# Two attentions of a two-block transformer on row halves of the array, with other places for a head's extras and a token-major key norm

## The reference

```python
s = einsum("bqhcd,bkhcd->bhcqk", q, k) * 64 ** -0.5
p = softmax(s)
w = p[:, :, 0] - lam * p[:, :, 1]
o = einsum("bhqk,bkhd->bqhd", w, v)                # v: 128 wide
o = o * rsqrt(mean(o * o) + 1e-5) * g * (1 - lam_init)
```

```python
q, k = rms_norm(heads(a_q), q_norm_g), rms_norm(heads(a_k), k_norm_g)
outs, lses = zip(*[dilated_window_attention(q, k, v, rel_bias, w, d) for w, d in DILATED_PATTERNS])
```

## Time and profile before

| | before |
|---|---|
| median of 3 runs | 2809.41 us (2808.64 to 2809.75) |
| profiled execution: time, span | 2811.53 us, 2809.7 us |
| mean granted PE clock | 0.963 |
| PE / DVE / ACT / POOL busy | 89% / 38% / 21% / 2% |
| instructions | 23563 |

### The profile page before, as it was taken

How to read it: one execution, slowest core, us unless ns; L and a number is a source line. 1 busy time by engine, 2 the same in 40 slices (tenths; PEclk the granted TensorE clock), 3 DMA queues, 4 the chain that set the end, 5 groups by cost and what they waited for, 6 DMA issues and landing times.

```text
span 2809.7 us, 23563 instructions
## 1 busy us (share of the span) xinstructions
PE 2507.4 (89%) x9789; PEld 1379.9 (49%) x9789; DVE 1059.4 (38%) x1759; ACT 581.7 (21%) x912; POOL 54.2 (2%) x75
## 2 busy tenths in 40 slices
PE   6899998889999779999899989789888897979888
PEld 2344544458888648888645455433223232323323
DVE  3353346346665576665456673400101010110101
ACT  1110115332332242332234242300000000000000
POOL 2000000000000100000000000000000000000000
PEclk9999999899999889999899999899999999999999
DMA  8050231035554215554110110499999999999998
GB/s 325 0 179 16 67 107 73 0 114 201 192 181 154 71 64 200 190 188 138 63 47 31 44 33 7 195 382 413 401 405 396 409 406 411 393 414 398 404 405 339
DMA packets 184545, 594.22 MB, mean 211 GB/s; under 512 B 12450, under 2 KB 13984, under 8 KB 167926
## 3 DMA queue, kind: packets, MB, share of 16 engines
q1 hardware_dynamic: 180482, 581.14, 54.3%
q0 software_dynamic: 3648, 11.44, 1.2%
q10 hardware_dynamic: 308, 0.13, 0.0%
HBM read 590.54 MB, written 2.13 MB: 211 GB/s over the span
## 4 chain that ended last, share of the span: by engine, by line
PE 68%; DMA 18%; DVE 9%; ACT 3%; SPq 1%; issue 1%; POOL 0%; ACTq 0%; DVEq 0%
PE PS L611 12%; PE PS L784 8%; PE PS L786 8%; PE PS L785 8%; PE PS L149 7%; PE PS L1008 7%; DMA RING<-in_w_up_dram 6%; PE PS L992 5%; DMA RING<-in_w_gate_dram 3%; PE PS L1022 2%; DMA AT_e<-in_w_up_dram 2%; PE PS L524 2%; PE PS L687 2%; DMA HID_e<-in_w_up_dram 1%; DMA AT_e<-in_w_gate_dram 1%; PE PS L915 1%
## 5 line engine op out<-in xcount | busy, mean ns | idle before, releaser
L992 PE MATMUL PS<-RING,HID_e 128*64 128x512 f32 x1280 | 331.5, 597 | 66.7 <-DMA RING<-in_w_up_dram 39.1
L2125 DVE TENSOR_TENSOR TMP<-TMP,PS 128x512 f32<-128x512 f32 x32 | 20.6, 684 | 567.7 <-PE PS L992 567.7
L992 PEld LDWEIGHTS PS<-RING,HID_e 128*64 128x64 f32 x1280 | 104.0, 136 | 262.2 <-issue 139.6
L1490 DVE SCALAR_TENSOR_TENSOR TMP<-RING,MODC,TMP 128x512 f32<-128x512 f32 x224 | 168.4, 752 | 19.3 <-ACT TMP L1099 10.0
L1008 PE MATMUL PS<-RING,HID_e 128*64 128x512 f32 x632 | 155.7, 594 | 2.5 <-DMA RING<-in_w_down_dram 2.5
L611 PE MATMUL PS<-AT_a,RING 128*128 128x512 f32 x320 | 140.7, 598 | 0.0
L992 PE MATMUL PS<-XT,HID_e 128*64 128x512 f32 x312 | 106.8, 597 | 14.8 <-DMA XT<-in_w_up_dram 7.5
L992 PE MATMUL PS<-AT_e,HID_e 128*64 128x512 f32 x296 | 104.3, 597 | 15.9 <-DMA AT_e<-in_w_up_dram 9.9
L611 PE MATMUL PS<-AT_e,RING 128*128 128x512 f32 x256 | 111.9, 593 | 0.0
L784 PE MATMUL PS<-AH_b,WH_b 128*128 128x512 f32 x256 | 101.2, 395 | 3.6 <-DVE AL_b L1539 3.6
L784 PE MATMUL PS<-AH_d,WH_d 128*128 128x512 f32 x256 | 101.4, 396 | 3.3 <-DVE AL_d L1539 3.2
(11 more groups left out here) (415 smaller groups left out, 3960.5 us busy)
## 6 DMA issues: line engine op xcount, KB each, us to landing
RING<-in_w_gate_dram SPq DMA_DIRECT2D x82, 1024.0 KB, 17.2
RING<-in_w_down_dram SPq DMA_DIRECT2D x79, 1024.0 KB, 22.7
RING<-in_w_up_dram SPq DMA_DIRECT2D x78, 1024.0 KB, 18.5
RING<-in_mlp_w_dram SPq DMA_DIRECT2D x64, 1024.0 KB, 5.4
RING<-in_ada_w_dram SPq DMA_DIRECT2D x48, 1024.0 KB, 5.3
RING<-in_w_ada_dram SPq DMA_DIRECT2D x24, 1024.0 KB, 5.1
XT<-in_w_up_dram SPq DMA_DIRECT2D x21, 1024.0 KB, 18.5
AT_e<-in_w_down_dram SPq DMA_DIRECT2D x21, 1024.0 KB, 21.2
```

The source lines that it names most:

```text
L992: last = pe.matmul(b[64 * d:64 * d + 64, :], xv_[:, k, 64 * d:64 * d + 64], wv, start=k == 0, stop=k == 7)
L1490: dve.scalar_tensor_tensor(out=ada_tmp, in0=ring.view("ada", which, cb, k // 4)[:, k % 4, :], scalar=sil[:, c0 + step * k:c0 + step * k + ...
```

## The change

In the differential attention the queries are stored once (`Qf`); the scores of half c use array rows 64c to 64c+63, and the order of the four matmuls alternates between the halves, with a wait of PE on its own matmul where two halves share a bank. lam is stored negated; the mix takes p0 + p1 * (-lam * s0 / s1) without dividing by s0, and the epsilon of the norm is multiplied by s0 squared instead (guard, mean). Values, sums, root, reciprocal and spread, scale are placed at steps 1, 2, 3 of the next head and 0, 1 of the one after that.

In the dilated attention keys are projected first, with tokens on partitions; their norm is 8 values per token, applied in a broadcast multiplication, and four transposes and an ACT copy with the product of both gains bring them back. The queries are copied as they are; their row sums (matmuls with two columns) give 128x8 row scales, which the logit operation takes as a per-row scalar in place of 0.125. A step s is now a pair of heads and 128 queries: two logit matmuls on row halves, two logit operations and maxima, one negation, two exponentials, one reciprocal. Logits run two steps ahead, with four buffers. The values of a pair come channel-major from column halves (8 matmuls of 512 columns), the reciprocals are broadcast by 8 matmuls and copied by ACT, and one DVE product writes the out-projection's input; so the final transposes, copies and the 32 scalings are gone. On SP the keys' weights are loaded ahead of the queries'; POOL loads the biases into four buffers and no longer clears the zero halves.

```diff
         def pe_scores(pe, w, n):
...
-            for c in range(2):
-                o = 1536 * (n % 2) + 768 * c
-                lhs = Qz[c][:, h, qi * 128:(qi + 1) * 128]
-                for k0, k1 in (((0, 512), (512, 768)), ((0, 256), (256, 768)))[c]:
-                    last = pe.matmul(flat[:, o + k0:o + k1], lhs, Kf[:, h, k0:k1], start=True, stop=True)
+            for c, k0, k1 in ((0, 0, 512), (1, 0, 256), (1, 256, 768), (0, 512, 768)):
+                o, p = 1536 * (n % 2) + 768 * c, slice(64 * c, 64 * c + 64)
+                if k0 == 512:
+                    w.wait_ge(*T_att.at("bank", n))
+                last = pe.matmul(flat[:, o + k0:o + k1], Qf[p, h, qi * 128:(qi + 1) * 128], Kf[p, h, k0:k1],
+                                 start=True, stop=True)
+                if k1 == 256:
+                    last.then_inc(*T_att.up("bank", n))
...
-                if n >= 4 and n % 4 == 0:
+                if n >= 8 and n % 4 == 0:
+                    pe_att_spread(pe, w, n // 4 - 2)
+                elif n >= 4 and n % 4 == 1:
                     pe_att_values(pe, w, n // 4 - 1)
-                elif n >= 4 and n % 4 == 1:
+                elif n >= 4 and n % 4 == 2:
                     pe_att_sums(pe, w, n // 4 - 1)
-                elif n >= 4 and n % 4 == 2:
-                    pe_att_spread(pe, w, n // 4 - 1)
+            pe_att_spread(pe, w, 2)
             pe_att_values(pe, w, 3)
...
+        def pe_dil_logits(pe, w, s):
+            hp, i = s // 4, s % 4
...
+            for c, b in enumerate(bs):
+                p = slice(64 * c, 64 * c + 64)
+                pe.matmul(b, aq[p, hp, i * 128:(i + 1) * 128], ak[p, hp, :], start=True, stop=True).then_inc(
+                    *T_dil.up("logits", s, c))
...
+        def pe_dil_values(pe, w, hp):
...
+            for st in range(4):
+                for c in range(2):
+                    h = 2 * hp + c
+                    last = pe.matmul(b[64 * c:64 * c + 64, :], av[:, st, h * 64:(h + 1) * 64], PTs.of(h)[:, st, :],
+                                     start=st == 0, stop=st == 3)
+            last.then_inc(*T_dil.up("pv", hp))
+            b = banks.take(w, ("dspread", hp), (S_dil, "spread", hp))
+            w.wait_ge(*V_dil.at("recip", 4 * hp + 3))
...
+            for s in range(16):
+                if s < 14:
+                    pe_dil_logits(pe, w, s + 2)
+                pe_dil_turn(pe, w, s)
+                if s % 4 == 0 and s:
+                    pe_dil_values(pe, w, s // 4 - 1)
+            pe_dil_values(pe, w, 3)
...
         def dve_att_mix(dve, w, n):
...
-            dve.tensor_tensor(st[:, 7:8], st[:, 7:8], lam, ALU.mult).then_inc(*V_att.up("mix", n, 1))
+            dve.tensor_scalar(st[:, 6:7], st[:, 6:7], st[:, 4:5], lam, ALU.mult, ALU.mult).then_inc(*V_att.up("mix", n, 1))
             w.wait_ge(*V_att.at("mix", n, 1))
-            dve.tensor_scalar(p1, p1, st[:, 7:8], None, ALU.mult).then_inc(*V_att.up("mix", n, 2))
-            w.wait_ge(*V_att.at("mix", n, 2))
-            dve.scalar_tensor_tensor(out=p0, in0=p0, scalar=st[:, 6:7], in1=p1, op0=ALU.mult, op1=ALU.subtract).then_inc(
+            dve.scalar_tensor_tensor(out=p0, in0=p1, scalar=st[:, 6:7], in1=p0, op0=ALU.mult, op1=ALU.add).then_inc(
...
         def dve_dilated(dve, w):
...
+            logits(0)
+            for s in range(16):
+                if s < 15:
+                    logits(s + 1)
+                w.wait_ge(*S_dil.at("exp", s, 1))
+                dve.reciprocal(soft(s, 3), soft(s, 2)).then_inc(*V_dil.up("recip", s))
+                if s % 4 == 0 and s:
+                    out(s // 4 - 1)
+            out(3)
```

More of the change, by code:

```diff
@@ L892, in pe_mlstm @@
                         last.then_inc(*T_ml.up("num", h, i, d))
[L894 to L906, removed]
@@ L908, in pe_dil_values, with pe_dil_rows @@
-        def pe_dil_values(pe, w, h):
-            b = banks.take(w, ("dpv", h), (V_dil, "scale", h, 3))
-            w.wait_ge(*S_dil.at("turn", 4 * h + 3))
-            w.wait_ge(*S_ml.at("av", 3))
-            pt = PTs.of(h)
-            for i in range(4):
[L914 to L917, removed]
+        def pe_dil_rows(pe, w, j):
+            b = banks.take(w, ("aq", "ss", j), (S_dil, "aq", "root", j))
+            w.wait_ge(*S_dil.at("aq", "sq", j))
+            q = act_tmp.of("aq", "sq", j)
+            for i in range(4):
+                last = pe.matmul(b[:, 2 * i:2 * i + 2], q[:, i * 128:(i + 1) * 128], half_sum, start=True, stop=True)
+            last.then_inc(*T_dil.up("aq", "ss", j))
@@ new lines, in pe_dil_turn @@
+        def pe_dil_turn(pe, w, s):
+            for c in range(2):
+                b = banks.take(w, ("dturn", s, c), (S_dil, "turn", s, c))
+                w.wait_ge(*S_dil.at("exp", s, c))
+                lg = lg_tmp.of("logit", s, c)
+                transposes(pe, b, [lg[:, st * 128:(st + 1) * 128] for st in range(4)]).then_inc(*T_dil.up("turn", s, c))
+        def pe_dil_values(pe, w, hp):
+            b = banks.take(w, ("dpv", hp), (V_dil, "out", hp))
+            w.wait_ge(*S_dil.at("turn", 4 * hp + 3, 1))
+            w.wait_ge(*S_ml.at("av", 3))
+            for st in range(4):
+                for c in range(2):
+                    h = 2 * hp + c
[4 more added lines that the diff above has]
+            w.wait_ge(*V_dil.at("recip", 4 * hp + 3))
+            for i in range(4):
+                for c in range(2):
+                    last = pe.matmul(b[64 * c:64 * c + 64, i * 128:(i + 1) * 128],
+                                     soft(4 * hp + i, 3)[:, c:c + 1].to_broadcast([128, 64]), ident[:, :],
+                                     start=True, stop=True)
+            last.then_inc(*T_dil.up("spread", hp))
@@ new lines, in pe_dil_keys, with pe_dil_key_turn @@
+        def pe_dil_keys(pe, w, i):
+            b = banks.take(w, ("ak", i), (V_dil, "ak", "mul", i))
+            for k in range(8):
+                w.wait_ge(*ring.landed("ak", k // 4))
+                last = pe.matmul(b, AT3[:, k, i * 128:(i + 1) * 128], ring.view("ak", k // 4)[:, k % 4, :],
+                                 start=k == 0, stop=k == 7)
+            last.then_inc(*T_dil.up("ak", i))
+        def pe_dil_key_turn(pe, w, i):
+            b = banks.take(w, ("kturn", i), (S_dil, "ak", "out", i))
+            w.wait_ge(*V_dil.at("ak", "mul", i))
+            q = dve_tmp.of("ak", i)
+            transposes(pe, b, [q[:, j * 128:(j + 1) * 128] for j in range(4)]).then_inc(*T_dil.up("kturn", i))
@@ L934, in pe_dilated @@
[L934 to L943, removed]
@@ L1349, in square @@
             def square(name, j):
-                q = act_tmp.take(w, (name, "sq", j), (T_dil, name, "ss", j))
+                q = act_tmp.take(w, (name, "sq", j), (V_dil if name == "ak" else T_dil, name, "ss", j))
                 w.wait_ge(*T_dil.at(name, j))
                 act.activation(q, banks.of(name, j), ACT.Square, bias=0.0, scale=1.0).then_inc(*S_dil.up(name, "sq", j))
[L1354 to L1373, removed]
@@ L1374, in act_dilated @@
-            exp(0)
[L1375 to L1384, removed]
-                act.activation(PTs.of(h)[:, :, i * 128:(i + 1) * 128],
-                               banks.of("dturn", n).rearrange("p (k n) -> p k n", n=128), ACT.Copy, bias=0.0,
-                               scale=1.0).then_inc(*S_dil.up("turn", n))
@@ new lines, in row_root, with exp @@
+            def row_root(j):
+                w.wait_ge(*T_dil.at("aq", "ss", j))
+                act.activation(row_scale(j), banks.of("aq", "ss", j)[:, 0:8], ACT.Sqrt, bias=eps64, scale=1.0).then_inc(
+                    *S_dil.up("aq", "root", j))
+            def exp(s):
+                for c in range(2):
+                    lg = lg_tmp.of("logit", s, c)
+                    w.wait_ge(*V_dil.at("neg", s))
+                    act.activation(lg, lg, ACT.Exp, bias=soft(s, 1)[:, c:c + 1], scale=1.0,
+                                   accum_out=soft(s, 2)[:, c:c + 1]).then_inc(*S_dil.up("exp", s, c))
@@ new lines, in spread @@
+            def spread(hp):
+                q = act_tmp.take(w, ("dspread", hp), (V_dil, "out", hp))
+                w.wait_ge(*T_dil.at("spread", hp))
+                act.activation(q, banks.of("dspread", hp), ACT.Copy, bias=0.0, scale=1.0).then_inc(
+                    *S_dil.up("spread", hp))
+            w.wait_ge(*V_dil.at("const"))
+            w.wait_ge(*V_dil.at("gain"))
+            for i in range(4):
+                square("ak", i)
+                w.wait_ge(*V_dil.at("ak", "ss", i))
+                act.activation(key_scale(i), key_scale(i), ACT.Sqrt, bias=epsc, scale=1.0 / 64).then_inc(
+                    *S_dil.up("ak", "root", i))
+                if i:
+                    key_out(i - 1)
@@ new lines, in act_dilated @@
+            for j in range(4):
+                square("aq", j)
+                act.activation(aq[:, j, :], banks.of("aq", j), ACT.Copy, bias=0.0, scale=1.0).then_inc(
+                    *S_dil.up("aq", "out", j))
```

(29 more changed lines are left out.)

221 lines of the change are left out of this document (112 added, 109 removed).

## The result

The changed kernel takes 2774.14 us (median of 4 runs, 2772.82 to 2776.89), the kernel before 2809.58 (median of 4): a ratio of 0.987, 95% interval 0.9853 to 0.9887. 2772 was forecast.

What follows compares the result with a forecast made beforehand. DVE was taken to set the attentions' steps, DMA the experts. 2811.5 less 21.9 (differential) and 15.4 (dilated) gave 2774.2; the median standing 2.1 under the profiled run, 2772 us was forecast, range 2757 to 2797.

Steps and rivals of the forecast that it cites:

- Plain step: Differential attention: folding the normalisation cuts DVE's step per 128 queries from 3.84 to about 3.2 us.
- Row halves run together: Differential attention scores: both array row halves start together, so a step's scores take about 1.4 us instead of 2.75.
- rival A: Both attentions: row halves run one after the other, scores stay at 2.6 to 2.75, total 2787 us; chance 0.16.
- Rival B: Both attentions: each change of array shape empties PE, 0.05 to 0.16 us each, total 2775 to 2782; chance 0.10.
- Extras spread out: Differential attention: values, sums, root and spread over later steps leave 9.4 us of stalls a head, not 12.3; head about 22.3.
- the tail: Differential attention, third values to out-projection: 28.9 us in place of 37.3, including 2.2 and 0.9 for half clock.
- The first values: Differential attention's start: first values at 437.2 in place of 439.09, despite waiting for one step more.
- the lower bound of 16: Differential attention's gain, forecast 21.9 us: 16 if the old stalls of 12.3 stay in two heads; upper bound 27.
- Rival C: Both attentions: granted clock stays at half throughout because PE has less to do, total 2845 us, slower; chance 0.05.
- Dilated attention: Its out-projection starts at 1699.3 in place of 1716.23; gain 15.4 us after 1.5 off for half clock; bounds 12 and 23.
- the new wait on DVE: Dilated attention: DVE idles 4.7 us before each of three pair products, waiting for values, spread and copy.
- So that last stretch has a fixed length.: Experts, from first expert load to the end: DMA-bound, fixed length, so time saved in the attentions is saved one for one.

Runs made afterwards that it cites:

- x5: The kernel before with only the folded mix, with its guard and mean; whole-row scores, old order of extras, old dilated part: 2799.16 us.
- x7: The changed kernel with three idle 128x512 matmuls on PE between the second and third scores of the differential attention; stage 107.9 us, whole time not given.
- x12: The changed kernel run again, unchanged: 2772.73 us.
- x1: The differential attention as changed, the dilated one as in the kernel before: 2800.56 us.
- x4: The changed kernel with DVE's product of a pair in the dilated attention one step later, behind the next logits: 2763.59 us.
- x10: The changed kernel with 112 matmuls of one column added behind the last values of the dilated part: 2829.37 us.
- x13: x4 with idle matmuls in two PE gaps near the dilated part's end: 2763.87 us, ratio 0.9841 to the kernel before.
- x9: x4 with a differential head's values placed behind the next step's scores and sums behind those after: 2767.31 us, ratio 0.9837.

## Why the prediction was right, and where it was wrong

The total was right, 2774.1 in a range of 2757 to 2797, but that was luck: the two attentions gave 9.5 less than forecast, and the last stretch 6.8 that nobody had forecast.

- **Plain step.** 3.2 forecast, 3.30 measured. Right; the mix made most of it (3.47 in x5, with the mix alone).
- **Row halves run together.** Right: in the dilated steps a pair of 64x512 takes 1.13 (four records), so rival A is out. But the scores take 1.89, not 1.4: I had left out the wait for the shared bank, and how much of the 0.5 it makes up no run isolates. The Trainium skill, "TensorEngine Tiling (Array Packing)", section Restrictions and Gotchas, says that two row tiles can't use one PSUM bank at once; the kernel keeps to it, and no run here tried without.
- **Rival B.** The first two records of a dilated pair end 0.70 after they start, against 0.59 for one in the experts:

```profile
1624.80 0.70 PE L919 MATMUL PS<-HID_e 64*128 64x512 f32 x2
```

  About 0.1 for the change into row halves, as priced. In the dilated steps these pairs run ahead of DVE, so there it costs next to nothing; where a maximum of the differential attention waits for scores it would be on the path. No run takes it out alone.
- **Extras spread out: this step failed.** Its waits were well priced (9.8 against 9.4 in the first head; 11.3 in the second, where the clock fell once more), and the root's 8.51 did go. But a head's period was put together from plain steps and waits alone. DVE's own guard, mean, reciprocal and scale (0.75 and three of about 0.1) and 0.1 a step were left out, and half clock was charged to the tail only. Counted from the first scores, the out-projection was forecast at 98.2 (510.7 - 412.5) and came at 107.8. The first values came at 28.1 against 24.7, and 1.9 of that is the half clock which x7 undid; the rest is not taken apart. The heads came out at 24.3 and 26.0 against 22.3, the tail at 29.4 against 28.9. In x12, with heads of 24.3 and 24.4, and in four others with this code (x1, x4, x10, x13) it is 104.7. So the gain of the stage is 12.3 to 15.4 in place of 21.9, at best just under the lower bound of 16.
- **Rival C in small.** The clock did fall in the steps, and never stayed at half for a whole stage. But it didn't come back with the values, as the argument from the earlier trace rows had it: in the stretches shown it rises between 420 and 424 and between 456 and 460, ahead of the values at 439.02 and 463.32, behind scores and transposes that kept PE busy for 4.00 of 4 us (452 to 456). Only the last values, from 505.97, saw it rise in their course (0.50 from 504, 0.95 from 508). The Trainium skill, "TensorE: Matmul & The Clock Gate", Part 1, says that the gate's window runs freely, so that the same kernel can meet its changes at other places in each run. The changed kernel's two executions agree with that: 107.8 and 104.7, with the clock at 0.57 from 484 to 488 in the first, and in x12

```profile
484.00:488.00 4.00, 3.56 (x22) 2.57 (x22) 2.44 (x4) 2.15 (x6) 0.00 (x0) 1.00 0.00 0
```

  Yet five of six executions with this code took the same 104.7.
- **Dilated attention.** 15.4 forecast, 13.9 measured. The mis-sized terms are its start and its end. The first negation came 1097.7 after the first out-projection, where the sum had 1095.6 (1628.2 - 532.6): the unchanged stages in between took 1.4 longer, and the second projection ran its first part at half clock (0.66 from 1557 to 1561), behind a wait that stood there before too. After, then before:

```profile
1556.37 1.09 PE L531 MATMUL PS<-ident,HID_e 128*128 128x128 f32 x4 [2.32 <-DVE HID_e L2055]
1557.25 8.27 PE L952 MATMUL PS<-RING,AT_e 128*128 128x512 f32 x16
```

```profile
1568.86 0.63 PE L524 MATMUL PS<-ident,HID_e 128*128 128x128 f32 x4 [2.33 <-DVE HID_e L1985]
1569.32 7.03 PE L611 MATMUL PS<-AT_e,RING 128*128 128x512 f32 x16
```

  From the first negation to the last 62.7 were forecast (46.5 + 16.2), and 61.8 measured; the new wait on DVE was 4.84 where 4.7 stood. The end is 7.9 from the last negation by forecast, measured 10.2, since the last values ran at half clock, 5.59 and not 3.65: x13, which undoes that on the kernel of x4, has 8.2. Together that is 3.5 late, of which 1.5 had been taken off for half clock; and the terms of the sum add up to 1698.8, not to 1699.3.
- **"So that last stretch has a fixed length."** That failed: it was 6.8 shorter, and made up for the attention. In the two kernels that were profiled twice it repeats within 2 us, and between kernels it differs by up to 10; what decides it is not settled.

## What to carry to other kernels

Build a period from everything that the bounding engine runs in it, small extras too, and ask what half clock would cost in each stage where a change leaves PE with less to do: row halves took 0.9 off PE's scores in each of 16 steps and returned 0.2 to 3.3 us in all, since PE was seldom last. A wait that a change puts on a busy queue can be worth moving one step later (x4: 7.7 us), but it can also only change places (x9). And measure the stage, not only the total: here two errors of 7 to 8 us hid each other.

## What was not expected of the hardware

Idle matmuls in a gap of 2 to 3 us speed up what follows: the scores from 3.37 to 1.89 (x7), the values from 6.20 to 3.65 (x13). In x7 the stage gained nothing by it. And the weight stream, 405 MB on the same instructions, took 1013.2 to 1023.1 us in fourteen profiled executions, within 2 us of itself in the two kernels that were profiled twice.
